# Turning the second heads of attention pairs right behind the first ones, in idle matmul banks of a one-core transformer kernel

## The chip, the cores and the metric

The kernel runs on 1 core of one Trainium2 chip. The metric is the device time of one execution in microseconds (us); that of a kernel is the median of several executions. TensorE, VectorE (DVE), ScalarE (ACT), GpSimd (POOL) and SyncE (SP) each take their own instructions strictly in order and meet at semaphores.

## The reference, cut to what matters

Three transformer layers at 256 tokens and width 2048, all in float32. The first block has a mixer (gated MLP, dilated attention, sparse attention), attention to a memory, and an MLP. The second block has two layers (l = 0, 1), and the change is in their mixers:

```python
proj = h @ w_in[l]                      # qa ka va qb kb vb qc kc vc, heads of 64
oa = window_attention(...)              # 8 heads, bias by distance, a sink
ob = neighborhood_attention(...)        # 8 heads, bias by position
oc = axial_global_attention(...)        # 16 heads, rotary, no bias
mix = concat(rmsnorm(oa), rmsnorm(ob), rmsnorm(oc))
x = x + mix @ w_o[l]
# then x = x + relu(rmsnorm(x) @ w_up)**2 @ w_down
```

Each attention is softmax(q k^T + bias) v. Heads are handled in pairs: 4 pairs of branch A, 4 of B and 8 of C in each layer.

## The kernel before, in words

A plan, `make_plan`, lists all steps in one order (`p.steps`), and every engine's program walks this list and issues its own part of each step. So the order of steps is the order of each engine's queue.

**Units.** The weights (600 MB) stream from HBM in halves of 128 x 1024 floats into five buffers `wt`. For exactness each half is split: ACT copies the high part to `wh` (L2173), VectorE forms the low part `wl` (L2435). TensorE multiplies: for each of 16 weight tiles one matmul with `wh` over 512 columns (high and low parts of the activations) and one with `wl` over 256. Sixteen such tiles are a unit, 32 matmuls. A unit adds up in one of three PSUM banks (0 to 2), taken in turn by `next_bank`; bank `banks["n"] % 3` is the next unit's. At the start of the next unit the sum is taken out: ACT copies one half of the bank to `tA`, VectorE adds the other into `tB`, GpSimd multiplies by the norm. Then the splits for the unit after follow. So the queues of ACT and VectorE hold, per unit: the sum of the last unit, two splits, and then the stage of attention.

**Order of units in a layer's mixer** (`ORDER2`): 4 value units `va`; tiles 26, 27 (keys of C); 18 to 25 (queries of C); 4 value units `vb`; tiles 4 (key of A), 0, 1, 2, 3 (queries of A), then 6, 10, 7, 11, 8, 12, 9, 13 (queries and keys of B in turn: tile 6+i is `qb` i, tile 10+i is `kb` i). A value unit holds two banks through all its four units. Then 8 units of two parts with the first half of `w_o`, and 8 with the second.

**Attention in the background.** Each pair is a generator, `two_heads`. `step_bg` runs at the eighth weight tile of a unit and lets each generator do one step, oldest pair first: load the biases (A and B alone, when two `sS` buffers are spare; there are six), two units of waiting, `score2`, then `prob`, then the turning, then `av`, in one unit each. At most one pair scores in a stage. In `score2` TensorE writes the scores of both heads, VectorE takes row maxima (L2579 for C, L2446 with the bias for A and B), ACT the exponentials (L2269, L2258). In `prob` VectorE takes a reciprocal and multiplies (L2595, L2439). Turning is four TensorE transposes of 128 x 128 for a head (L1827) and a copy of the bank to `sP`: on ACT for the first head (L2173), on VectorE for the second (L2749). `av` is the product with the values, eight matmuls of `sP`.

**Where the second head waits.** There is one bank for turning, `bP` (bank 5). So the first head is turned in the stage at tile 8, and the second is put into `late`, which runs at tile 13 of the same unit. Until the norm of C is formed, the second heads of A and B take `bM` (bank 7) instead.

```python
turn_head(hds[0], pts[0], 0)
late.append(lambda: turn_head(hds[1], pts[1], 1))
```

**B's masks.** A bias of B comes by eight small DMAs for a pair, issued by SP (L1810), and GpSimd adds a mask to it (L2794, `sS<-sS,c`), four instructions a pair, at the place of the bias step.

**The norm of C.** `across` forms it between two units: sums over the channels at tile 13 of one unit, then at tile 3 of the next one TensorE spreads the result over the bank `bM` and VectorE copies it to `rB`. Until then no sum of a unit is taken out (`held["evac"]`). The norm of the memory in the first block goes the same way.

Of the kernel before, what the change touches and what calls it, by code (L numbers as in the profile page):

```python
# [53 lines left out]
class Plan:  # L54
# [9 lines left out]
    def step(self, *what):  # L64
        self.steps.append(what)
# [76 lines left out]
def make_plan():  # L142

    p = Plan()
# [91 lines left out]
    held = {"evac": False, "s1": 0}  # L236

    late = []
# [40 lines left out]
    def run_at13():  # L279
        while at13:  # L280
            at13.pop(0)()
# [8 lines left out]
        else:  # L290
            step("mm", h, k, k + 1)

    banks = {"n": 0, "held": set()}

    def next_bank():

# [51 lines left out]

    def unit_end():
        run_at13()  # L350
        while after_unit:
            after_unit.pop(0)()

# [19 lines left out]
    def unit(parts, nk, src, thin=False, stages=(8,), ahead=2, early=False, tail=False):  # L373

        u = unit_begin(ahead)
        n = 0
        for j, (first, last, ev) in enumerate(parts):
            if first:
                next_bank()
            g = len(groups) - 1  # L380
            for k in range(nk):
                marks(n, None if len(parts) == 1 else max(1, 4 - n // 4) if thin else 0, stages, early)
                if (thin or tail) and n == 11:
                    run_pending()
                h = where[2 * u + n // 8][1]
                end = last and k == nk - 1
                if thin:
                    half = 2 * k // nk
                    tiles[h].append((g, src(j, k % (nk // 2)), k % (nk // 2) == 0, end, half, (k + 1) % (nk // 2) == 0))
                else:  # L390
                    tiles[h].append((g, src(j, k), first and k == 0, end, None, end))
                matmuls(h, n % 8)
                if n % 8 == 7:
                    done[g] = tick("t_used", h)
                    give(("wh", h % 4), done[g])
                elif end:
                    done[g] = tick("t_thin", g)
                n += 1
            if last:
                pending.append((ev, g))  # L400
                if j < len(parts) - 1:
                    kept = pending.pop()
                    run_pending()
                    pending.append(kept)
        unit_end()
        return done[g]

# [27 lines left out]
    def value_unit(name, ev, stages=(8,), ahead=2, early=False):  # L435

        v = VALUES[name]
        u = unit_begin(ahead)
        if name not in open_values:
            gs = next_bank(), next_bank()  # L440
            banks["held"] |= {p.bank[g] for g in gs}
            open_values[name] = [*gs, 0]
        g0, g1, k = open_values[name]
        n = 0
        for c in range(2):
            h = where[2 * u + c][1]
            for i in range(v.depth):
                for q in range(2):
                    for _ in range(4 // v.depth):
                        marks(n, None, stages, early)  # L450
                        n += 1
                    step("vmm", h, (g0, g1)[q], q, src_x(k), i, v.width, k == 0, k == KT - 1, (c, i, q) == (c, v.depth - 1, 1))
                k += 1
            done[g0] = done[g1] = tick("t_used", h)
            give(("wh", h % 4), done[g1])
        open_values[name][2] = k
        if k == KT:
            del open_values[name]
            banks["n"] = 3 - p.bank[g0] - p.bank[g1]
            pending.append((ev, (g0, g1)))  # L460
        unit_end()
        return done[g1]
# [106 lines left out]
    def across(begin, end):  # L569

        kept = {}

        def first():
            kept["b"] = begin()
            held["evac"] = True

        def second():
            end(kept["b"])
            held["evac"] = False
            run_pending()  # L580
        at13.append(first)
        after_unit.append(lambda: at3.append(second))

    def end_T(b, scale=None, keep=False):
        norm_end(b, "rT", scale, keep)
# [553 lines left out]

    sS_of, qden, branch_norms = {}, {}, set()  # L1140

    def turn_head(hd, pt, j):
        s = sS_of[hd]
        apart = j == 1 and hd[1] in "AB" and (hd[0], "C") not in branch_norms
        bank = "bM" if apart else "bP"
        step("turn", hd, s, pt, j, apart)
        take(bank, bank, *hd)
        take(("Pt", pt), "Pt", *hd)
        give(("S", s), tick("t_turn", *hd))
        sS.held.discard(s)  # L1150
        give(bank, tick("v_pcopy" if j else "a_pcopy", *hd))

    def av_heads(pr, parts):
        step("av", pr, tuple(parts))
# [37 lines left out]
    def two_heads(pr, qk, v, bias=False, sink=False):  # L1192

        hds = [(*pr, j) for j in range(2)]
        if bias:
            while sS.spare() < 2:
                yield
            for hd in hds:
                s = sS_of[hd] = sS.grab()
                step("bias", hd, s)  # L1200
                take(("S", s), "S", *hd)
                if hd[1] == "B":
                    tick("g_mask", *hd)
            yield
            yield
        else:
            while not has("g_rope", *qk[0], 1):
                yield
            yield
        while (held["s1"] >= 1 or dens.spare() < 4 or not (bias or sS.spare() >= 2)  # L1210
               or not all(has("g_proj", *x) or has("v_rdone", *x) or has("g_rope", *x, 1) and x[0] == "qc" for x in qk)):
            yield
        held["s1"] += 1
        ds = [dens.grab() for _ in hds]
        dq = None if bias else qden[qk[0][1]]
        if not bias:
            for hd in hds:
                s = sS_of[hd] = sS.grab()
                take(("S", s), "S", *hd)
        step("score2", pr, tuple(sS_of[hd] for hd in hds), tuple(ds), bias, sink, dq)  # L1220
        for j, (hd, d) in enumerate(zip(hds, ds)):
            take(("bS", j), "bS", *hd)
            take(("den", d), "den", *hd)
            tick("t_score", *hd)
            if bias:
                tick("v_max", *hd, 0)
                give(("bS", j), tick("v_max", *hd, 1))
                if sink:
                    tick("v_max", *hd, 2)
            else:  # L1230
                tick("v_max", *hd, 0)
                tick("v_max", *hd, 1)
            for n_ in range(3 if sink else 2):
                tick("a_exp", *hd, n_)
            if not bias:
                give(("bS", j), ("a_exp", at["a_exp", *hd, 1]))
        if dq is not None:
            give(("den", dq), ("a_exp", at["a_exp", *hds[1], 1]))
            dens.held.discard(dq)
        yield  # L1240
        for hd, d in zip(hds, ds):
            prob_ticks(hd, d, sink)
        yield
        while sP.spare() < 2:
            yield
        pts = [sP.grab() for _ in hds]
        turn_head(hds[0], pts[0], 0)
        late.append(lambda: turn_head(hds[1], pts[1], 1))
        yield
        while not has("a_v", *v):  # L1250
            yield
        av_heads(pr, [(hds[j], pts[j], j, v) for j in range(2)])
# [150 lines left out]
    for l in range(2):  # L1403
# [90 lines left out]
        for t in ORDER2:  # L1494
# [3 lines left out]
            if t >= 26:  # L1498
                ev = rope_tile("kc2", t - 26, G_QK2 + 2 + l, 64.0 ** -0.5)
            elif t >= 18:  # L1500
                ev = rope_tile("qc", t - 18, G_QK2 + l, None)
            elif t >= 10:
                ev = project("kb", (l, t - 10), free="o2")
            elif t >= 6:
                ev = project("qb", (l, t - 6), "Q", free="o2")
            elif t == 4:
                ev = project("ka", (l, 0), free="o2")
            else:
                ev = project("qa", (l, t), "Q", free="o2")
            last_in = unit([(True, True, ev)], KT, X2)  # L1510
            if 18 <= t < 26:
                pair("C", t - 18)
            elif t == 4:
                for br in "AB":
                    for i in range(4):
                        pair(br, i)
# [38 lines left out]
def program(nc, I, out):  # L1555
    p, feed, tiles, done = make_plan()
    at, free = p.at, p.free
    with ExitStack() as ctx:
# [261 lines left out]
        def _(eng):  # L1820
# [254 lines left out]
                    t = mm(bS[b][:, qt * T:(qt + 1) * T], q[b0:b0 + n, qt * P:(qt + 1) * P], k[b0:b0 + n, 0:T], True, True)  # L2075
                t.then_inc(S.t_score)

            def prob_turn(hd, s, pt, odd, apart):
                w.wait_ge(S.v_prob, at["v_prob", *hd])
                bank = bM if apart else bP  # L2080
                let_go(w, "bM" if apart else "bP", *hd)
                for kt in range(2):
                    for qt in range(2):
                        t = turn(bank[:, kt * T + qt * P:kt * T + (qt + 1) * P], sS[s][:, qt, kt * P:(kt + 1) * P])
# [346 lines left out]
        def _(eng):  # L2431
# [183 lines left out]
            for kind, *key in p.steps:  # L2615
# [126 lines left out]
                elif kind == "prob":  # L2742
                    prob(*key)
                elif kind == "turn" and key[3]:
                    hd, s, pt, _, apart = key
                    bank = bM if apart else bP
                    w.wait_ge(S.t_turn, at["t_turn", *hd])
                    let_go(w, "Pt", *hd)
                    eng.tensor_copy(sP[pt][:, :, :], bank[:, 0:512].rearrange("p (a b) -> p a b", a=2)).then_inc(S.v_pcopy)  # L2749
# [338 lines left out]
```

## Time and profile before

| | |
|---|---|
| median of 3 runs | 3294.0 us (3291.27 to 3294.38) |
| the profiled execution | 3291.06 us, span in the profile 3289.3 us |
| TensorE busy | 99% of the span, granted clock 0.999 |
| VectorE, ACT, GpSimd busy | 66%, 49%, 28% |
| DMA | 604.55 MB, mean 184 GB/s |
| C stretch, first layer | about 1257 to 1337 us |
| C stretch, second layer | about 2295 to 2373 us |
| the A and B tiles behind it | 1337 to 1429, 2373 to 2464 us |

All times in the rows are microseconds from the start of the span, unless marked ns. A busy TensorE isn't TensorE at its peak: matmuls overlap, and their ends are modelled, so the starts are the better measure. "[0.51 <-DVE sP L2749]" at a row's end says that the engine was idle for 0.51 us ahead of it and what ended that.

### The profile page before, as it was taken

The page shows a single profiled execution, that of the slowest core. Times are in us where ns is not written, and L with a number is a line of the kernel's source. Part 1 is how long each engine was busy: PE and PEld are TensorE (multiplying, and loading weights), DVE is VectorE, ACT ScalarE, POOL GpSimd, SP SyncE. Part 2 cuts the span into 40 slices and gives each one's busy share as a digit, 9 for nine tenths or more (in the row PEclk, how much of TensorE's full clock was granted, in tenths as well). Part 3 has the DMA queues.
Part 4 walks back from the last instruction along what each step waited for, and adds up shares of the span by engine and source line. Part 5 has one row for each costly group of instructions (what it writes and reads, how often), then busy time and mean ns, then how long its engine had stood idle before and what let it go on. Part 6 is the DMA issues. An engine that isn't in the chain of part 4 may idle for free.

```text
span 3289.3 us, 48362 instructions
## 1 busy us (share of the span) xinstructions
PE 3261.1 (99%) x19088; PEld 2854.0 (87%) x19088; DVE 2174.3 (66%) x3068; ACT 1621.1 (49%) x2692; POOL 915.6 (28%) x821
## 2 busy tenths in 40 slices
PE   8999999999999999999999999999999999999998
PEld 7989888888888897788888888889788888888887
DVE  6668687754676668778764477555778775457654
ACT  5457454443444545555443344444655544344443
POOL 2434133210232224255320033112336331013221
PEclk9999999999999999999999999999999999999999
DMA  7544546756655553555565566555355565555554
GB/s 259 189 165 149 176 157 216 230 191 191 191 189 193 185 188 132 161 168 184 192 192 193 186 188 190 194 190 178 125 176 170 187 190 195 190 186 190 189 193 145
DMA packets 188279, 604.55 MB, mean 184 GB/s; under 512 B 36597, under 2 KB 41573, under 8 KB 188054
## 3 DMA queue, kind: packets, MB, share of 16 engines
q1 hardware_dynamic: 188054, 601.47, 56.8%
q8 instruction: 151, 2.47, 0.3%
q14 instruction: 74, 0.61, 0.1%
HBM read 599.16 MB, written 8.00 MB: 185 GB/s over the span
## 4 chain that ended last, share of the span: by engine, by line
PE 91%; DVE 5%; ACT 2%; issue 1%; POOL 0%; DMA 0%; DVEq 0%; POOLq 0%; SPq 0%; ACTq 0%
PE ps L1824 90%; DVE wl L2435 3%; ACT sS L2269 1%; PE ps L1827 1%; DVE x L2443 1%; ACT wh L2173 1%; DVE xr L2435 1%; DVE sS L2439 1%; DVE den L2579 0%; ACT tA L2173 0%; DMA wt<-in_w_in 0%; POOL acc L2794 0%; DVE ua L2443 0%; POOL qc L2794 0%; ACT tG L2426 0%
## 5 line engine op out<-in xcount | busy, mean ns | idle before, releaser
L2435 DVE TENSOR_TENSOR wl<-wt,wh 128x1024 fp32r<-128x1024 f32 (+2 forms) x1104 | 1469.1, 1363 | 311.5 <-ACT wh L2173 295.5
L1824 PE MATMUL ps<-x,wh 128*128 128x512 f32 x4448 | 1561.8, 393 | 11.8 <-DVE x L2443 9.8
L1824 PE MATMUL ps<-x,wl 128*128 128x256 f32 x4448 | 1254.5, 282 | 0.0
L2173 ACT ACTIVATE wh<-wt 128x1024 fp32r<-128x1024 f32 (+2 forms) x1104 | 1117.8, 1051 | 275.0 <-PE ps L1824 235.8
L1824 PEld LDWEIGHTS ps<-x,wh 128*128 128x128 f32 x4448 | 836.1, 188 | 192.3 <-DVE wl L2435 12.8
L1824 PEld LDWEIGHTS ps<-x,wl 128*128 128x128 f32 x4448 | 841.8, 189 | 0.6
L1824 PE MATMUL ps<-ua,wh 128*128 128x512 f32 (+1 forms) x2432 | 832.0, 386 | 0.0
L1824 PE MATMUL ps<-ua,wl 128*128 128x256 f32 x2368 | 667.4, 282 | 0.0
L2435 DVE TENSOR_TENSOR tB<-ps,tA 128x256 f32<-128x256 f32 x422 | 177.1, 423 | 724.1 <-ACT tA L2173 723.9
L2173 ACT ACTIVATE tA<-ps 128x256 f32<-128x256 f32 x422 | 158.8, 380 | 943.0 <-PE ps L1824 942.8
L1824 PE MATMUL ps<-ub,wh 128*128 128x512 f32 x1536 | 536.6, 390 | 0.0
L1824 PEld LDWEIGHTS ps<-ua,wh 128*128 128x128 f32 x2432 | 452.2, 188 | 92.7 <-issue 1.4
L2794 POOL TENSOR_TENSOR tB<-tB 128x256 f32<-128x256 f32 x192 | 316.8, 1650 | 735.7 <-DVE tB L2443 735.7
L1824 PEld LDWEIGHTS ps<-ua,wl 128*128 128x128 f32 x2368 | 447.5, 189 | 0.2
L1824 PE MATMUL ps<-ub,wl 128*128 128x256 f32 x1536 | 433.1, 282 | 0.0
L2794 POOL TENSOR_TENSOR xr<-xr,tB 128x256 f32<-128x256 f32 x143 | 118.5, 831 | 858.2 <-DVE tB L2435 855.7
L1824 PEld LDWEIGHTS ps<-ub,wh 128*128 128x128 f32 x1536 | 288.3, 188 | 60.4
L1824 PEld LDWEIGHTS ps<-ub,wl 128*128 128x128 f32 x1536 | 290.3, 189 | 0.0
L2794 POOL TENSOR_TENSOR acc<-acc,tS 128x256 f32<-128x256 f32 x122 | 153.1, 1255 | 111.5 <-ACT tS L2178 102.5
L1824 PE MATMUL ps<-wh,x 128*128 128x512 f32 (+3 forms) x512 | 145.5, 358 | 0.5 <-DVE wl L2435 0.5
L1824 PEld LDWEIGHTS ps<-wh,x 128*128 128x128 f32 x512 | 91.8, 188 | 13.6 <-issue 2.1
L1824 PE MATMUL ps<-wl,x 128*128 128x512 f32 (+3 forms) x256 | 90.4, 353 | 0.0
(233 smaller groups left out, 1843.2 us busy)
## 6 DMA issues: line engine op xcount, KB each, us to landing
wt<-in_w_up SPq DMA_DIRECT2D x384, 512.0 KB, 4.4
wt<-in_w_down SPq DMA_DIRECT2D x384, 512.0 KB, 4.7
wt<-in_w_in SPq DMA_DIRECT2D x156, 512.0 KB, 4.6
wt<-in_w_o SPq DMA_DIRECT2D x64, 512.0 KB, 4.5
wt<-in_w_out SPq DMA_DIRECT2D x32, 512.0 KB, 4.5
wt<-in_w_vb SPq DMA_DIRECT2D x16, 512.0 KB, 4.0
wt<-in_w_va SPq DMA_DIRECT2D x16, 384.0 KB, 3.7
wt<-in_w_vsl SPq DMA_DIRECT2D x8, 512.0 KB, 6.2
```

The lines of the kernel that those rows point to most:

```text
L1824: return eng.matmul(o, l, r, start=start, stop=stop, skip_group_check=True)
L1827: return eng.transpose(o, i, idt[0:n, 0:n])
L2173: return eng.activation(o, i, ACT.Copy, **kw)
L2269: eng.activation(sS[s][:, qt, :], bS[b][:, qt * T:(qt + 1) * T], ACT.Exp, bias=nm[:, qt:qt + 1], scale=scale, accum_out=dn[:, qt:qt + 1]). ...
L2435: return eng.tensor_tensor(o, a, b, op)
L2439: return eng.tensor_scalar(o, a, s1, None, op0)
L2443: return eng.scalar_tensor_tensor(out=o, in0=a, scalar=s, in1=b, op0=op0, op1=op1, **kw)
L2794: return eng.tensor_tensor(o, a, b, op)
```

## The change

Four things. The second head is turned in the same stage, directly behind the first, if `idle_bank` finds one of the three matmul banks that neither the open unit nor a sum not yet taken out occupies. It finds none while sums are held back (`evac`), in units of two parts, and in unit 25, which stands ahead of value units (`fresh`); then the second head goes into `late` as before. For A and B it looks first at the next unit's bank, for C first at the one after that, which is the last unit's. The copy by VectorE then reads that bank, and the bank's next user waits for this copy. Last, the second half of `across` runs at tile 5 instead of tile 3.

```diff
+    def idle_bank(older):
+
+        if held["evac"] or banks["open"] is None or banks["fresh"]:
+            return None
+        busy = set(banks["open"])
+        for _, g in pending:
+            busy |= {p.bank[i] for i in (g if isinstance(g, tuple) else (g,))}
+        left = [(banks["n"] + j) % 3 for j in ((1, 0, 2) if older else (0, 1, 2)) if (banks["n"] + j) % 3 not in busy]
+        return left[0] if left else None
...
     def unit_end():
         run_at13()
+        banks["open"] = None
...
+            banks["open"] = (p.bank[g],) if len(parts) == 1 else None
...
+        banks["open"] = (p.bank[g0], p.bank[g1])
...
         at13.append(first)
-        after_unit.append(lambda: at3.append(second))
+        after_unit.append(lambda: at5.append(second))
...
-    def turn_head(hd, pt, j):
+    def turn_head(hd, pt, j, b=5):
         s = sS_of[hd]
-        apart = j == 1 and hd[1] in "AB" and (hd[0], "C") not in branch_norms
-        bank = "bM" if apart else "bP"
-        step("turn", hd, s, pt, j, apart)
-        take(bank, bank, *hd)
+        bank = {5: "bP", 7: "bM"}.get(b, ("main", b))
+        step("turn", hd, s, pt, j, b)
+        take(bank, "turn", *hd)
         take(("Pt", pt), "Pt", *hd)
         give(("S", s), tick("t_turn", *hd))
         sS.held.discard(s)
         give(bank, tick("v_pcopy" if j else "a_pcopy", *hd))
+
+    def second_turn(hd, pt):
+        b = idle_bank(hd[1] == "C")
+        if b is not None:
+            turn_head(hd, pt, 1, b)
+        else:
+            late.append(lambda: turn_head(hd, pt, 1, 7 if hd[1] in "AB" and (hd[0], "C") not in branch_norms else 5))
...
         turn_head(hds[0], pts[0], 0)
-        late.append(lambda: turn_head(hds[1], pts[1], 1))
+        second_turn(hds[1], pts[1])
...
+            banks["fresh"] = t == 25
             last_in = unit([(True, True, ev)], KT, X2)
+            banks["fresh"] = False
```

## Rows read from the trace of the kernel before

**Rows 1.** The page: the span, and TensorE's busy time, share and instructions.
```profile
span 3289.3 us, 48362 instructions
...
PE 3261.1 (99%) x19088; PEld 2854.0 (87%) x19088; DVE 2174.3 (66%) x3068; ACT 1621.1 (49%) x2692; POOL 915.6 (28%) x821
```

**Rows 2.** TensorE's waits over the whole span: us in total, times, longest.
```profile
PE ps L1824 <- DVE sP L2749: 0.9, 2, 0.5
PE ps L1827 <- ACT sP L2173: 0.7, 2, 0.4
```

**Rows 3.** Timeline of TensorE, C stretch: start, us, operation [idle before <-releaser].
```profile
1284.56 1.08 PE L1824 MATMUL ps<-sP,vc 128*64 128x256 f32 x4
1286.15 1.08 PE L1824 MATMUL ps<-sP,vc 128*64 128x256 f32 x4 [0.51 <-DVE sP L2749]
...
1295.47 1.81 PE L1824 MATMUL ps<-sP,vc 128*64 128x256 f32 x8
...
1325.04 1.09 PE L1824 MATMUL ps<-sP,vc 128*64 128x256 f32 x8
...
1337.71 0.63 PE L1827 MATMUL ps<-idt,sS 128*128 128x128 f32 x4 [0.36 <-ACT sP L2173]
```

**Rows 4.** The chain of waits in order of time: start, us, what.
```profile
1287.15 0.96 ACT wh L2173
1288.13 2.98 DVE wl L2435 x2
...
1297.27 0.96 ACT wh L2173
...
1333.39 1.16 ACT vb L2173 x2
...
1343.77 1.75 PE ps L1824 x10
1345.52 0.44 PE ps L1827 x4
```

**Rows 5.** Timeline of VectorE, end of the C stretch.
```profile
1339.64 0.68 DVE L2749 COPY sP<-ps 128x512 f32<-128x512 f32 x1
1340.24 0.41 DVE L2435 TENSOR_TENSOR tB<-ps,tA 128x256 f32<-128x256 f32 x1
```

**Rows 6.** Timeline of TensorE, value products of A0 and A3.
```profile
1377.83 1.59 PE L1824 MATMUL ps<-sP,va 128*64 128x256 f32 x8
...
1416.01 1.88 PE L1824 MATMUL ps<-sP,va 128*64 128x256 f32 x8
```

**Rows 7.** Timeline of VectorE, units 6 and 10.
```profile
1377.60 0.69 DVE L2749 COPY sP<-ps 128x512 f32<-128x512 f32 x1
...
1380.49 2.51 DVE L2435 TENSOR_TENSOR wl<-wt,wh 128x1024 fp32r<-128x1024 f32 x2 [0.53 <-ACT wh L2173]
```

**Rows 8.** Timeline of SP's DMA issues, biases of B0 and B2.
```profile
1387.86 6.33 SPq L1810 DMA_DIRECT2D sS<-rpm  x8
...
1420.26 5.20 SPq L1810 DMA_DIRECT2D sS<-rpm  x8
```

**Rows 9.** Timeline of GpSimd, masks of the same pairs (B0: second head).
```profile
1396.43 1.23 POOL L2794 TENSOR_TENSOR sS<-sS,c 128x256 f32<-128x256 f32 x2 [0.64 <-DMA sS<-rpm]
...
1425.06 3.52 POOL L2794 TENSOR_TENSOR sS<-sS,c 128x256 f32<-128x256 f32 x4 [4.57 <-DMA sS<-rpm]
```

**Rows 10.** Timeline of TensorE, the spread of C's norm.
```profile
1438.50 0.63 PE L1824 MATMUL ps<-idt,den 128*128 128x128 f32 x4
```

**Rows 11.** Timeline of VectorE, the read of C's norm.
```profile
1440.02 0.42 DVE L2483 COPY rB<-ps 128x256 f32<-128x256 f32 x1
```

**Rows 12.** Timeline of VectorE, prob products with GpSimd idle and while it masks.
```profile
1365.24 0.62 DVE L2439 TENSOR_SCALAR sS<-sS,den 128x256 f32<-128x256 f32 x2
...
1404.51 1.14 DVE L2439 TENSOR_SCALAR sS<-sS,den 128x256 f32<-128x256 f32 x2
```

**Rows 13.** Busy time, C stretch: length, each engine, clock, DMA share, GB/s.
```profile
1257.90:1337.70 79.80, 78.66 (x437) 59.67 (x437) 62.11 (x137) 49.38 (x119) 30.15 (x32) 1.00 0.34 113
```

More of the change, by code:

```diff
@@ L291, in matmuls @@
             step("mm", h, k, k + 1)
-    banks = {"n": 0, "held": set()}
+    banks = {"n": 0, "held": set(), "open": None, "fresh": False}
+    def idle_bank(older):
[6 more added lines that the diff above has]
+        return left[0] if left else None
     def next_bank():
@@ L2076, in score, with prob_turn @@
                 t.then_inc(S.t_score)
-            def prob_turn(hd, s, pt, odd, apart):
+            def prob_turn(hd, s, pt, odd, b):
                 w.wait_ge(S.v_prob, at["v_prob", *hd])
-                bank = bM if apart else bP
-                let_go(w, "bM" if apart else "bP", *hd)
+                bank = ps[:, b, :]
+                let_go(w, "turn", *hd)
                 for kt in range(2):
@@ L2744, in _ @@
                 elif kind == "turn" and key[3]:
-                    hd, s, pt, _, apart = key
-                    bank = bM if apart else bP
+                    hd, s, pt, _, b = key
+                    bank = ps[:, b, :]
                     w.wait_ge(S.t_turn, at["t_turn", *hd])
```

## The prediction

> **What bounds the kernel now.** I read the page first: TensorE is busy for 99% of the span [rows 1], so time comes or goes only where TensorE waits or is given other work. The matmul work is the same after the change, so I looked for waits. The view of TensorE's waits gives the copies of turned heads (`sP`) 1.6 us in two rows, over both layers [rows 2]. That understates them, because matmul ends are modelled. The timeline shows more: the eight matmuls of a value product take 1.09 us where all is ready (1325.04), but four of them took 1.59 us (1284.56 to 1286.15), against half of that, and eight took 1.81 us at 1295.47 [rows 3]. So some 1.1 and 0.7 us were lost waiting for the second head's copy on VectorE, which stands at the end of VectorE's stage. These are the waits that the change goes at.
>
> The second thing to see is the chain of waits through the C stretch, about 1257 to 1337 us. It doesn't run through TensorE. It goes round ACT and DVE: first half of `wh` at 1287.15, both `wl` at 1288.13, then the prob products, the row maxima, the exponentials, and the next `wh` at 1297.27 [rows 4]. One round is 10.1 us and nothing in it waits for TensorE; both engines take their instructions in order. It ends in the copies of `vb` (1333.39 to 1334.55) and, after `wh`, the copy of a turned head, for which TensorE's turning at 1337.71 waits [rows 3]. TensorE has nearly as much work per round as the loop is long, so it is 99% busy and still follows the loop.
>
> **The change, part by part.** I call a unit by its tile number. Pair Ci scores in unit 22+i for i up to 3, then in the four `vb` units; it is turned two units later and multiplied with its values three units later.
>
> 1. *Turning itself.* No instruction is added. Four turns between weight matmuls take 0.44 us in the chain [rows 4], and eight in a row should take twice that; I count 0.
>
> 2. *The second head's copy on VectorE, C pairs.* Before, it came after the row maxima, while ACT did exponentials: outside the loop. Now its step stands before the prob products and maxima of younger pairs, so it is inside. Two instructions after each other show its price: 1339.64 to 1340.24, 0.60 us [rows 5]. An idle bank is found for pairs 0, 2, 3, 4, 5 before the last exponentials of the stretch (pair 1 is held back in unit 25): 5 x 0.60 = 3.0 us on the loop. TensorE gains the lost waits of value products but runs into the loop again: turning pair 6 in unit 4 takes a bank that has just held `vb`, and must wait for the copies of `vb`. These now end at 1334.55 + 3.0 = 1337.55. Then four turns 0.44 and ten matmuls 1.75 with 0.09 for the switch [rows 4] bring TensorE to 1339.8, where it was at 1338.1 (1337.71 and 0.4 for the turns). That is +1.7 us a layer. Bounds: -0.4 (only the wait of 0.36 goes [rows 3]) and +2.1 (five copies at their whole 0.68 [rows 5]).
>
> 3. *Waits of value products, A and B pairs.* The product of A0 takes 1.59 us (1377.83), that of A3 1.88 (1416.01) [rows 6]; 1.09 would do, and the next group starts 0.07 before its end. Both wait for a copy that VectorE reaches late (1377.60 [rows 7]). With the copy ahead of the prob products both go: -0.5 - 0.8 = -1.3 us. Bounds: 0 and -1.3.
>
> 4. *The bank taken.* For A and B the idle bank is the next unit's, so the next unit's first matmul waits for the copy. Behind A1 (unit 10) that bites. TensorE: turning at 1377.83 + 1.02 = 1378.85, two heads 0.88, 16 matmuls 2.8 with 0.1 [rows 4], so unit 7 could start at 1382.6. VectorE: `wl` at 1380.49, pushed by A0's copy to 1381.1, ends 1383.6 [rows 7], and the copy behind it at 1384.2. Wait: +1.6 us. For the other pairs the copy is in time by the same count, by only 0.4 us for A0. Bounds: 0.6 (no push, and VectorE's `wl` at its shortest) and 2.5.
>
> 5. *What else the turn gives back.* An `sS` buffer is free in the plan once its head is turned. Now both of a pair's are free in the same stage, before younger pairs are asked, so from A3 on each bias load, score, prob and turn comes one unit earlier. B3's bias is loaded in unit 12 instead of 13, and its masks on GpSimd stand ahead of the product of key tile `kb` 2, for which B2's score in unit 9 waits. SP may issue these loads when B0 is turned in unit 12. From SP's first issue to the last mask's end it took 8.3 us once (1420.26 to 1428.58) and 9.8 once (1387.86 to 1397.66) [rows 8, 9]; the key's product adds 0.74. TensorE needs 2.8 + 2.8 + 1.0 + 0.9 = 7.5 us from that turn to B2's score. So it waits 8.3 + 0.74 - 7.5 = 1.5 to 3.0 us. I take 1.6, near the short end, since the shorter row is from the units nearest to it. Bounds: 0, if the key is formed in time, and 3.0. Below the masks nothing is saved, since the scores are only moved.
>
> 6. *The norm's spread at 5 instead of 3.* In the C norm it was on TensorE at 1438.50, and VectorE read it at 1440.02, behind `wl` [rows 10, 11]. Two tiles (0.7 us) later it ends at about 1439.6, still ahead of the read. Cost 0; if that cover were gone, 0.7 us of evacuation, still ahead of the bank's next use. The norm of the memory lies the same way.
>
> Per layer: +1.7 - 1.3 + 1.6 + 1.6 = +3.6; two layers +7.2 us. The profiled execution took 3291.1 us (span 3289.3 and 1.8 around it), so +7.2 makes 3298.3. It lies 2.9 below the median of the runs, 3294.0; on that the forecast is 3301.
>
> One rule bears on item 5. Two prob products of one head take 0.62 us at 1365.24 and 1.14 us at 1404.51, where GpSimd was masking [rows 12]. The Trainium skill, page SBUF — State Buffer, section "SBUF: two separate sides", says that VectorE and GpSimd share a port pair, which is held for a whole instruction while the other is fully blocked; this trace agrees in direction. By it the masks, coming one unit earlier, would slow other VectorE work instead. The number of masks stays, and I add nothing.
>
> **The rivals.**
> *A: the loop is not lengthened.* VectorE has idle time in each round, and if the copy fills it, waits vanish and nothing comes for them. For it: DVE is busy for only 62 of 80 us in the stretch [rows 13]. Against it: the chain has no gap in which it could hide. It gives -1.1 - 0.7 - 0.4 in the C stretch and -1.3 after it, -3.5 a layer, 3287. It decides for faster from the point where items 4 and 5 together cost under 1.8 us a layer.
> *B: TensorE's new waits are hidden.* The loop is longer, but the key comes in time and the bank is free nearly in time (0.6): 1.7 - 1.3 + 0.6 = +1.0 a layer, 3296.
> *C: all terms at their upper ends.* 2.1 - 1.3 + 2.5 + 3.0 = +6.3 a layer, 3307.
> *D: the change does nothing.* No idle bank is found or the plan is the old one. The code excludes it for single-tile units.
>
> **How the numbers follow.** What a measurement here can tell from no change is 0.2%, 6.6 us. The forecast (+3 to +11 us) has 0.48, A (3283 to 3291) 0.17, B (3291 to 3297) 0.27, C 0.08. The range reaches from half of A to C: 3288 to 3307; the likeliest case alone has 3297 to 3305. A is faster in most of its span, with a little for what I have not seen: 0.17. Slower by over 0.2% is C and two thirds of the forecast's case: 0.41. The rest, 0.42, is within.
>
> **What would show it.** Loop: rounds in the C stretch of 10.7 instead of 10.1 us, `vb` copies 3 us later against the stretch's start. Item 2: value products of 1.02 us, and turning of pair 6 behind the copies of `vb`. Item 4: a gap ahead of unit 7's first matmul, released by the copy. Item 5: A3's score one unit earlier and a gap ahead of B2's score, released by GpSimd. The prediction is wrong if VectorE's order lets the copy slip beside the exponentials, if `wl` gets shorter because fewer of them meet GpSimd, or if the bias loads land faster with a less crowded queue.

## The result and the profile after

The changed kernel takes 3306.08 us (median of 5 runs, 3304.92 to 3309.68), the kernel before 3294.0 (5 runs beside it, 3291.27 to 3294.52). The ratio is 1.004, interval 1.0029 to 1.0051: slower. The forecast was 3301. 3306 lies in the range of 3288 to 3307, but near its upper end, and beyond 3297 to 3305, the range of the likeliest case. "Within 0.2%" had been given 0.42 and "slower" 0.41, so, by the forecast's own threshold of 0.2%, the likelier of these two did not happen.

The profiled execution took 3306.08 us, 15.0 more than the profiled one of before. The page of the changed kernel, for [rows 1]:

```profile
span 3304.3 us, 48374 instructions
...
PE 3260.5 (99%) x19088; PEld 2855.8 (86%) x19088; DVE 2171.9 (66%) x3068; ACT 1620.4 (49%) x2692; POOL 910.4 (28%) x821
```

The matmuls are the same in number, and summed over the kernel their busy time is too, so all 15 us show as gaps. Not all of it was caused by waits: the groups of value products are 8.2 us shorter in all (44.1 before, 35.9 after), and other groups are longer by about as much, in part where the granted clock was low. The view of TensorE's waits, for [rows 2] (us in total, times, longest):

```profile
PE ps L1845 <- DVE x L2464: 9.9, 2, 9.0
PE ps L1845 <- POOL kb L2815: 8.0, 4, 3.4
PE ps L1845 <- DVE sP L2770: 4.1, 5, 1.7
PE ps L1848 <- DVE tB L2456: 3.8, 2, 2.9
PE ps L1845 <- DVE wl L2456: 2.4, 4, 0.8
PE ps L1848 <- ACT vb L2194: 2.4, 2, 1.2
```

Of these the first and the fifth were there before as well. New are the waits for keys that GpSimd forms (`kb`, 8.0), more waits for the VectorE copy (`sP`, 4.1), one in each layer for the last unit's sum (`tB`, 3.8), and pair 6's for `vb` (2.4). In place of [rows 3] and [rows 6], the timeline of TensorE:

```profile
1276.68 0.60 PE L1848 MATMUL ps<-idt,sS 128*128 128x128 f32 x4
1280.14 1.09 PE L1848 MATMUL ps<-idt,sS 128*128 128x128 f32 x4 [2.86 <-DVE tB L2456]
1281.16 2.09 PE L1845 MATMUL ps<-kc,qc 64*128 64x256 f32 x8
...
1289.55 1.09 PE L1845 MATMUL ps<-sP,vc 128*64 128x256 f32 x8
...
1337.45 0.66 PE L1848 MATMUL ps<-idt,sS 128*128 128x128 f32 x4
1339.29 0.63 PE L1848 MATMUL ps<-idt,sS 128*128 128x128 f32 x4 [1.18 <-ACT vb L2194]
...
1381.09 1.09 PE L1845 MATMUL ps<-sP,va 128*64 128x256 f32 x8
...
1387.65 0.47 PE L1845 MATMUL ps<-x,wh 128*128 128x512 f32 x1 [1.67 <-DVE sP L2770]
...
1409.39 1.14 PE L1845 MATMUL ps<-kb,qb 64*128 64x256 f32 x8 [1.14 <-POOL kb L2815]
...
1416.21 1.09 PE L1845 MATMUL ps<-sP,va 128*64 128x256 f32 x8
...
1428.30 1.14 PE L1845 MATMUL ps<-kb,qb 64*128 64x256 f32 x8 [2.39 <-POOL kb L2815]
...
2464.62 1.09 PE L1848 MATMUL ps<-idt,sS 128*128 128x128 f32 x8
2469.09 2.09 PE L1845 MATMUL ps<-kb,qb 64*128 64x256 f32 x8 [3.37 <-POOL kb L2815]
```

The value products are at 1.09 where they took 1.6 to 1.9 before: what the change goes at, it gets. In return each of the new waits stands where a step of the prediction had put one, and two stand where none had: the second turn of pair 0 at 1280.14, and the score at 1409.39 (key tile 1). Two of the scores also take 2.09 instead of 1.14 us. There the granted clock was at the lower of its two levels, 1.2 instead of 2.4 GHz. The view of the windows (length, busy us of PE, PEld, DVE, ACT, POOL, then the granted clock, DMA share, GB/s):

```profile
496.00:500.00 4.00, 3.35 (x11) 2.99 (x12) 3.61 (x6) 1.19 (x2) 0.90 (x2) 0.50 0.46 157
...
1280.00:1284.00 4.00, 3.86 (x17) 2.75 (x18) 3.45 (x5) 1.92 (x3) 1.05 (x2) 0.57 0.20 27
...
2464.00:2468.00 4.00, 1.72 (x16) 1.03 (x12) 1.97 (x3) 1.15 (x3) 2.12 (x4) 1.00 0.71 134
2468.00:2472.00 4.00, 2.91 (x11) 2.10 (x12) 0.84 (x5) 0.37 (x1) 1.67 (x3) 0.50 0.74 304
2472.00:2476.00 4.00, 4.00 (x17) 3.43 (x17) 0.63 (x4) 1.83 (x9) 0.00 (x0) 0.65 0.01 2
```

A stretch at clock c loses its length times (1 - c), if TensorE sets the pace there: the last two rows 4 x 0.50 + 4 x 0.35 = 3.4 us.

To place the rest I took the same instruction in both traces and subtracted the times. This is the lag behind the kernel before, in us, for all kernels of this study, under the names that they have in the experiments below; the column heads are the second C score of the layer's mixer (start of C in layer 0), the last C value product, the first C score of layer 1, its last C value product, the last matmul that reads `wh`, and the end of the span. All 14 come from one profiled execution each.

```
              C0 start  C0 end  C1 start  C1 end  last wh   end
before (at)    1267.6   1349.7   2297.5   2385.4   3275.4  3289.3
after             1.9      3.3      6.5      7.4     14.5    15.0
norm3             2.6      3.2      8.1      8.9     14.0    14.6
hold_s            1.2      2.6      5.1      5.9      8.1     9.1
hold_bank         0.8      2.2      3.7      4.5      6.4     7.2
best3             0.8      1.5      3.3      3.5      5.4     5.9
ab_only           0.0      0.0      3.3      3.3      8.9     9.3
a_only            1.7      1.7      2.6      2.6      3.5     3.5
b_only            0.2      0.3      1.3      1.3      2.3     3.3
c_only            0.3      1.7      1.7      2.5      2.7     3.1
c_not24           1.4      2.1      2.1      2.3      2.5     2.5
c_late            1.2      3.5      4.3      5.3      5.4     5.4
c_1to4            1.6      3.1      3.5      4.4      4.6     5.0
c_1to5            1.0      3.1      3.0      4.5      4.6     4.5
```

So of the changed kernel's 15.0 us, C took 1.4 and 0.8 in the two layers, A and B 3.3 and 7.1. The end of the kernel, behind the last weights, took 0.5; it varies from 0 to 1.0 among these executions and is no part of A and B. The 1.9 ahead of the mixer of layer 0 is no part of the change's cost: there the clock fell at 492 to 504 us, which it did in 7 of the 14 profiled executions (after, norm3, hold_s, a_only, c_not24, c_late, c_1to4), and these came 1.2 to 2.6 late, the others 0 to 1.0. The five runs of the kernel before also fall into two groups, 3291.3 to 3291.7 and 3294.0 to 3294.5.

### The profile page after: what moved, and what is told of

Read it like the earlier page. It is cut to its first block, busy times and chain, and to the rows that moved or that the text cites. A ratio compares the mean times of both kernels' runs of the same rounds, so it can differ in the third digit from the quotient of the medians.

```text
span 3304.3 us, 48374 instructions
## 1 busy us (share of the span) xinstructions
PE 3260.5 (99%) x19088; PEld 2855.8 (86%) x19088; DVE 2171.9 (66%) x3068; ACT 1620.4 (49%) x2692; POOL 910.4 (28%) x821
## 4 chain that ended last, share of the span: by engine, by line
PE 87%; DVE 6%; ACT 4%; issue 2%; POOL 1%; DMA 0%; SPq 0%; DVEq 0%; POOLq 0%; ACTq 0%
PE ps L1845 86%; DVE wl L2456 3%; ACT wh L2194 1%; ACT sS L2290 1%; DVE sS L2460 1%; ACT sS L2279 1%; PE ps L1848 1%; POOL acc L2815 0%; DVE x L2464 0%; DVE xr L2456 0%; DVE den L2600 0%; DVE sP L2770 0%; ACT tA L2194 0%; DMA sS<-rpm 0%; DVE sS L2467 0%
```

## The experiments

The kernel before, run again beside the experiments, had medians of 3292.1 to 3292.7 (15 to 33 runs each). All are the changed kernel with the edit shown.

### One part undone: held buffers, and the norm

```diff
     def second_turn(hd, pt):                        # hold_s
...
             turn_head(hd, pt, 1, b)
+            s = sS_of[hd]
+            sS.held.add(s)
+            late.append(lambda: sS.held.discard(s))
```

> The changed kernel, but a second head's buffer `sS` counts as free in the plan only at tile 13, as in the kernel before; the turn itself stays early. Theory (step 5 of the prediction, mis-sized): the waits for key tiles 1 and 2 behind GpSimd's masks (1.1 and 2.4 us in layer 0, 1.2 and 3.4 in layer 1) go, and with them the half-clock stretch behind the last one; 3306 - 8 - 2 = about 3296. Rival (steps 2 and 4, the VectorE copy on the loop and the bank waits are the cost, step 5 costs nothing): 3303 or more.

Measured: 3298.78 us, ratio 1.002 (1.0011 to 1.0029). 7.3 us of the 13.6 are gone (the changed kernel's 3306.1 less 3292.5, the kernel before in its largest set, 33 runs), and the four waits for `kb` with them. The theory's sum said 10. What it missed is in the waits of hold_s. The first matmul of the unit behind A1 still waits for the copy, as in the changed kernel. With the scores back at their old places, the units behind A3 and B0 wait for it too (the second and third row), which the key waits had hidden.

```profile
1386.92 0.47 PE L1848 MATMUL ps<-x,wh 128*128 128x512 f32 x1 [1.65 <-DVE sP L2773]
...
1417.74 0.47 PE L1848 MATMUL ps<-x,wh 128*128 128x512 f32 x1 [0.63 <-DVE sP L2773]
...
1426.59 0.47 PE L1848 MATMUL ps<-x,wh 128*128 128x512 f32 x1 [1.02 <-DVE sP L2773]
```

By the table A and B now take 2.5 and 2.2 us, instead of 3.3 and 7.1: in layer 0 the key waits of 3.5 us cost 0.8 net, in layer 1 those of 4.5 us cost 4.9, of which 3.4 was the clock.

```diff
-        after_unit.append(lambda: at5.append(second))
+        after_unit.append(lambda: at3.append(second))      # norm3
```

> The changed kernel with the third branch's norm spread back at tile 3. Theory (step 6: free): 3306 within 2. Rival (the later spread costs the 1.9 us by which the changed kernel is later before layer 0's mixer, or frees or delays something at the branch end): 3303 or less.

Measured: 3305.68 us, ratio 1.004 (1.0028 to 1.0053), 0.4 under the changed kernel. The later spread is free, as said. Its trace serves for the clock. Here it fell in layer 0 behind a wait of 2.36 us, where the changed kernel's wait of 2.39 at the same instruction left it up. From norm3, TensorE's timeline and the windows:

```profile
1428.28 1.56 PE L1845 MATMUL ps<-kb,qb 64*128 64x256 f32 x8 [2.36 <-POOL kb L2815]
```

```profile
1424.00:1428.00 4.00, 1.92 (x16) 1.16 (x13) 1.91 (x3) 1.15 (x3) 3.21 (x5) 1.00 0.81 215
1428.00:1432.00 4.00, 3.72 (x15) 2.81 (x16) 1.47 (x8) 1.75 (x7) 0.86 (x2) 0.61 0.54 217
1432.00:1436.00 4.00, 4.00 (x24) 3.51 (x23) 1.06 (x2) 2.34 (x5) 0.74 (x1) 0.96 0.00 0
```

That is 4 x 0.39 + 4 x 0.04 = 1.7 us, and A and B take 8.1 - 3.2 = 4.9 there, 1.6 more than in the changed kernel.

### One part alone: C, A, B

```diff
-        b = idle_bank(hd[1] == "C")
+        b = idle_bank(True) if hd[1] == "C" else None          # c_only
+        b = None if hd[1] == "C" else idle_bank(False)         # ab_only
+        b = idle_bank(False) if hd[1] == "A" else None         # a_only
+        b = idle_bank(False) if hd[1] == "B" else None         # b_only
```

> Early second turns for the third branch (C) alone; A's and B's are turned at tile 13 as before. Theory: C's own cost is the wait in unit 24 with its half-clock stretch and pair 6's wait for copies, less the value product waits: +1.4 in layer 0 and +0.9 in layer 1, so 3294 + 2.3 = about 3296 (3294 to 3299). Rival (the loop of ACT and VectorE lengthened by the copies is the main cost): 3300 or more.

> Early second turns for branches A and B alone; C's at tile 13 as before. Theory: A and B carry the main cost, +3.9 in layer 0 and +7.9 in layer 1: 3294 + 9 to 12 = 3303 to 3306. Rival (C's turns are the main cost): 3298 or less.

Measured: c_only 3294.63 us, ratio 1.0007 (0.9999 to 1.0016), 2.5 above the kernel before. ab_only 3301.67, ratio 1.0029 (1.0018 to 1.004), 9.6 above it. These fit the expected 2.3 and 9 to 12 above the kernel before. Together they are 12.1 of the 13.6, so the two nearly add up, and about three quarters belong to A and B.

> Early second turns for branch A alone. Theory of step 5 (A's freed buffers bring A3's score and B1's forward, and their keys are late behind the masks on GpSimd): A's early turns carry the key waits, 1.1 and 2.4 us or more in layer 0, and the copy wait of 1.7 a layer; 3299 to 3302, most of the 9.6 of A and B together. Rival (B's turns free the buffers that matter): 3294 to 3296, no key wait above 0.5.

> Early second turns for branch B alone. A's alone cost 2.0 us (3294.7), A's and B's together 9.6 (3301.7). Theory (the wait for key tile 2 needs both: A's early turns bring the scores forward and B's bring B3's buffers, biases and masks in front of that key on GpSimd): B alone costs little, 0 to 3 us, 3292.5 to 3295.5, and no score waits over 1 us for a key. Rival (B's early turns put the masks in front of the key by themselves): 3297 to 3300, with the wait of 2 to 3 us in both layers.

Measured: a_only 3294.70 us, ratio 1.0006 (0.9997 to 1.0015), 2.0 above. b_only 3294.50, ratio 1.0005 (0.9996 to 1.0014), 1.9 above. Neither interval is clear of 1, but both are far below the 9.6 of A and B together. So my theory for a_only fell: A's early turns bring the wait for key tile 1 (1.22 in layer 0, 0.94 in layer 1) and the copy wait of 1.66, but most of the 9.6 us isn't theirs. The rival there was wrong about the key wait, right about the time. The theory for b_only held: it has no wait for a key, and the wait for key tile 2 needs both. The wait for key tile 1 has another cause than the theories gave. In the changed kernel GpSimd had finished its masks and stood idle until VectorE's sum of that unit came; the score had moved up to where its key was only being formed:

```profile
1408.56 0.73 POOL L2815 TENSOR_TENSOR kb<-tB,rT 128x256 f32<-128x256 f32 x1 [3.41 <-DVE tB L2456]
```

For key tile 2 GpSimd's timeline shows the masks. In a_only the key (1421.97) comes before the masks of B3 (1428.41 and 1430.53):

```profile
1421.97 1.65 POOL L2815 TENSOR_TENSOR kb<-tB,rT 128x256 f32<-128x256 f32 x1 [1.42 <-DVE tB L2456]
...
1428.41 1.23 POOL L2815 TENSOR_TENSOR sS<-sS,c 128x256 f32<-128x256 f32 x2 [3.13 <-DMA sS<-rpm]
```

In the changed kernel all four masks of B3 stand in front of it (for [rows 9]), and the load that they wait for is issued one unit earlier than before, right behind B0's turn. GpSimd's timeline, and SP's of both layers (for [rows 8]):

```profile
1424.79 2.73 POOL L2815 TENSOR_TENSOR sS<-sS,c 128x256 f32<-128x256 f32 x4 [2.57 <-DMA sS<-rpm]
1427.48 0.72 POOL L2815 TENSOR_TENSOR kb<-tB,rT 128x256 f32<-128x256 f32 x1
```

```profile
1418.89 5.20 SPq L1831 DMA_DIRECT2D sS<-rpm  x8
...
2458.68 5.20 SPq L1831 DMA_DIRECT2D sS<-rpm  x8
```

### The bank, and unit 24

```diff
-        b = idle_bank(hd[1] == "C")
+        b = idle_bank(True)                        # hold_bank: hold_s and this
...
-            banks["fresh"] = t == 25
+            banks["fresh"] = t in (24, 25)         # c_not24: c_only and this; best3: all three
```

> The kernel with the held buffers (3298.8), and A's and B's second turns go to the bank that the unit after the next takes, as C's do, so that the next unit's first matmul doesn't wait for the copy. Theory (step 4): of the waits for that copy, 5.9 us in all over the kernel before, four of 1.0 to 1.7 and one of 0.6 go; 3298.8 less 5 to 6 = 3293 to 3294. Rival (the waits come back at another place, the other bank being still read by the last unit's sum): 3297 or more.

Measured: 3298.74 us, ratio 1.0017 (1.0008 to 1.0026), the same as hold_s. The rival held. The waits for the copy fall from 6.8 to 1.1 us in all, but the other bank has not been read yet when the turn wants it, and the turns now wait for the last unit's sum, 8.9 us in all instead of 3.9. TensorE in hold_bank:

```profile
1373.24 0.63 PE L1851 MATMUL ps<-idt,sS 128*128 128x128 f32 x4 [0.46 <-DVE tB L2459]
...
1382.87 0.63 PE L1851 MATMUL ps<-idt,sS 128*128 128x128 f32 x4 [0.56 <-DVE tB L2459]
...
1413.22 0.63 PE L1851 MATMUL ps<-idt,sS 128*128 128x128 f32 x4 [1.47 <-DVE tB L2459]
```

Its profiled execution has shorter A and B stretches (1.5 and 1.9 us, against 2.5 and 2.2) and no clock fall before the last units, but its median is not below that of hold_s.

> Early second turns for the third branch alone, but not in unit 24 either, where pair 0 is turned while the last unit's sum is still due. Theory (the wait of 2.9 us for that sum with the half-clock stretch behind it, and 1.0 in layer 1, is C's cost; elsewhere C gains the value product waits less pair 6's): 3294.6 of the third-branch kernel less 4 to 5 = 3290 to 3291, 1 to 2 under the kernel before. Rival (C's cost is the copies on the loop of ACT and VectorE, step 2): no gain over 3294.6.

Measured: 3293.92 us, ratio 1.0002 (0.9993 to 1.0011), 0.7 under c_only, which is not clear of noise, where 4 to 5 were expected. The theory fell. By the table C takes 1.4 and 0.8 us with the early turn in unit 24 and 0.8 and 0.2 without, and that difference of 0.6 is the copy on the loop, not the wait: the round of ACT at this place takes 10.09 us in c_only and 9.50 in c_not24, as in the kernel before. ACT in c_only and in c_not24:

```profile
1277.83 2.00 ACT L2194 ACTIVATE wh<-wt 128x1024 fp32r<-128x1024 f32 x2
1287.92 1.99 ACT L2194 ACTIVATE wh<-wt 128x1024 fp32r<-128x1024 f32 x2
```

```profile
1278.91 2.00 ACT L2194 ACTIVATE wh<-wt 128x1024 fp32r<-128x1024 f32 x2
1288.41 1.99 ACT L2194 ACTIVATE wh<-wt 128x1024 fp32r<-128x1024 f32 x2
```

TensorE's wait of 2.9 us itself is made good within the next units, where the value products no longer wait: in c_only the lag behind the kernel before is 3.9 us right behind it and 0.8 by 1300 us. A clock fall of 1.7 us there is absorbed as well. c_only had one behind this wait and hold_bank had none; yet both are 1.4 us later at the end of C than at its start. In a_only it fell at 1280 us with no early turn near, and the lag was 1.7 before and after. norm3 lost 3.4 us there, and C took 0.6. TensorE is not what sets the pace in this stretch.

> All three edits: held buffers, the other bank for A and B, no early turn in unit 24. If the three costs add up: 3293.5 less 4 to 5 = 3289, which is 3 under the kernel before (the value product waits of A0, A3 and C go and nothing comes in their place but pair 6's 1.2 us). If they hide one another: 3292 or more.

Measured: 3296.85 us, ratio 1.0012 (1.0003 to 1.0021). The waits hide one another: with all three edits the early turns are still 4.3 us worse than none, as the second of the two expectations (3292 or more) had it.

### C: the copies on the loop

```diff
         give(("S", s), tick("t_turn", *hd))
...
-        give(bank, tick("v_pcopy" if j else "a_pcopy", *hd))
+        def copied():                              # c_late: c_only and this
+            if j:
+                step("copy2", hd, pt, b)           # VectorE's part alone
+            give(bank, tick("v_pcopy" if j else "a_pcopy", *hd))
+        if b in (5, 7):
+            copied()
+        else:
+            late.append(copied)
```

> Early second turns for the third branch alone, in the same units, but only TensorE's part is early: VectorE's copy of the second head stays at tile 13. Theory of step 2 (the early copies lengthen the loop of ACT and VectorE and make pair 6's turn wait for copies of vb, 1.2 us a layer): pair 6's wait falls to 0.4 or less, about 1.7 us a layer less, 3291 to 3293; the value products wait again as in the kernel before if the late copy is what held them, which would take some 1.3 to 3 back. Rival (the loop isn't lengthened by the copies): pair 6 still waits 1.2 and the time stays at 3294.6 or goes above it.

Measured: 3294.99 us, ratio 1.0005 (0.9996 to 1.0014), not below c_only. Neither the theory nor the rival has both right: the mechanism is there, the time is not. ACT's timeline shows the loop. The changed kernel, for [rows 4]:

```profile
1299.67 2.00 ACT L2194 ACTIVATE wh<-wt 128x1024 fp32r<-128x1024 f32 x2
1310.41 2.00 ACT L2194 ACTIVATE wh<-wt 128x1024 fp32r<-128x1024 f32 x2
...
1337.87 1.27 ACT L2194 ACTIVATE vb<-ps,den 128x512 f32<-128x512 f32 x2
```

and c_late:

```profile
1299.93 2.00 ACT L2201 ACTIVATE wh<-wt 128x1024 fp32r<-128x1024 f32 x2
1309.54 2.00 ACT L2201 ACTIVATE wh<-wt 128x1024 fp32r<-128x1024 f32 x2
...
1335.74 1.27 ACT L2201 ACTIVATE vb<-ps,den 128x512 f32<-128x512 f32 x2
```

From the `wh` of this round to the copies of `vb` it is 38.2 us with the copies early and 35.8 with them late; before it was 1333.4 - 1297.3 = 36.1 [rows 4]. So four early copies (of pairs 2 to 5) put 2.1 us on the loop. In four rounds they added 0.6, 0.6, 0.3 and 0.6, by ACT's timelines of both kernels. Pair 6's wait for `vb` is gone from c_late's waits. What probably eats the gain: this execution had the longest clock fall of all at 1276 to 1292 us (0.88, 0.50, 0.50 and 0.84 in four windows of 4 us, 5.1 us lost), so its layer 0 can't be compared with the others as a whole; and in layer 1 the bank is wanted before the late copy has read it:

```profile
2372.53 0.47 PE L1852 MATMUL ps<-x,wh 128*128 128x512 f32 x1 [1.38 <-DVE sP L2777]
```

Last, I tried to keep the part of C in which the lag had shrunk (from 1.3 to 0.3 us over pairs 0 to 4 in c_not24, before it grew to 2.1):

```diff
+        b = idle_bank(True) if hd[1] == "C" and 1 <= hd[2] <= 4 else None      # c_1to4; c_1to5: <= 5
```

> Early second turns for pairs 1 to 4 of the third branch alone. In the kernel with all but pair 0 early (3293.9) the lag behind the kernel before fell by 1.0 us from pair 1 to pair 4 in layer 0 and by 1.5 in layer 1, and grew by 1.8 in each from pair 5 on, where the second turn waits for copies of vb. Theory: the growth goes, the gain stays, 2.5 us under the kernel before: 3289 to 3291 against 3292.5. Rival (the 1.8 is only work moved back to its place, owed anyway once the early turns stop): 3292 to 3294.

> The same with pair 5 early too, whose copy the next unit's first matmul waits 0.3 us for. Theory (pair 5 costs 0.3 to 0.9 a layer by its copy on the loop and that wait, pair 6 the rest): 0.6 to 1.8 above the run of pairs 1 to 4. Rival (only pair 6 costs): no more than 0.3 above it.

Measured: c_1to4 3295.36 us, ratio 1.001 (1.0001 to 1.0019); c_1to5 3298.08, ratio 1.0015 (1.0007 to 1.0024). My theory fell: stopping early doesn't keep the gain. With pair 5 the median is 2.7 above that of pairs 1 to 4, more than the 0.6 to 1.8 expected; the two profiled executions don't show this difference, since that of c_1to5 was its fastest run (3295.6). TensorE is ahead only for a few units, and meets the longer loop at the next place where it needs a copy. In c_1to4 that is the late turn of pair 6, which waits for ACT's copy; in c_1to5 it is the same one with a longer wait:

```profile
1340.81 0.63 PE L1848 MATMUL ps<-idt,sS 128*128 128x128 f32 x4 [1.37 <-ACT sP L2194]
```

```profile
1340.82 0.63 PE L1848 MATMUL ps<-idt,sS 128*128 128x128 f32 x4 [2.46 <-ACT sP L2194]
```

No version here beats the kernel before.

## Why the prediction was off

The sum was +7.2 us, measured +12 beside it and +13.6 against the later runs of before. The costs that the forecast named are all in the trace. The step that failed is the size of item 5, the waits for keys: 3.5 and 4.5 us were measured where 1.6 a layer was put in. The lowered clock behind the longest of these waits, 3.4 us, was not in the sum at all.

- *Item 1, turning itself: right.* Eight turns take 1.02 to the next group.
- *Item 2, copies on the loop, +1.7 a layer: right in mechanism, in size for layer 0 alone.* C took 1.4 and 0.8 us (also in c_only). A round with an early copy takes 10.74 us (1299.67 to 1310.41), where the same round took 10.14 before, as forecast (10.7). Counted from the start of C, the `vb` copies come 2.7 us later (3.0 forecast), and pair 6's turn waits 1.18 for them. c_late confirms it from the other side. In layer 1 the `vb` copies come 8.7 us later than before (2377.65 against 2368.97) where C began 6.5 later, 2.1 of its own. Rival A, that the copies fill idle time, is thereby excluded in both layers. I did not see that pair 0's turn, in unit 24, would wait 2.86 us for a sum; it made no difference to the time, and the 0.6 a layer that c_not24 saves is pair 0's copy on the loop.
- *Item 3, the value products of A0 and A3, -1.3 a layer: right,* at 1381.09 and 1416.21, where both end after 1.02 us.
- *Item 4, the bank, +1.6: right, in part by luck.* The wait ahead of unit 7 is 1.67 and 1.64 us. But "for the other pairs the copy is in time" held only because the key waits came first: in hold_s, without them, the waits for the copy are 3.3 and 2.7 us.
- *Item 5, +1.6 a layer, upper bound 3.0: too small.* First, a wait was missed: A3's early turn brings B1's score forward too, and key tile 1, held up by VectorE's sum and not by masks, is late for it by 1.14 and 1.15 us. Second, the wait for key tile 2 is 2.39 and 3.37 us. From the end of B0's turn (1418.25) to the score (1428.30) it took 10.05 us: 0.64 until SP issued, 8.63 from there to the last mask's end, 0.78 for the key. I had 8.3 and 0.74, from the shorter of two rows, and nothing between turn and issue. In layer 1 the same path took 11.04 (0.63, 9.6 and 0.8); the longer row, 9.8, was the one to take there. TensorE's 7.5 us between them was right (7.67). So item 5 was 3.5 and 4.5 us instead of 1.6. With items 3 and 4 that makes 3.8 and 4.8 a layer; measured without the clock, 3.3 and 3.7.
- *Not in the sum: the clock.* Behind the 3.37 us wait in layer 1 the granted clock fell and took 3.4 us. With it A and B make 7.1 us of that layer in the table. In ab_only it was 1.7 us at the same place, and 5.6 less 1.7 is 3.9, much the same.
- *Item 6, the norm, 0: right* (norm3).

By layer the forecast had 3.6 and 3.6, of which A and B 1.9 each; the trace has 4.7 and 7.9, A and B 3.3 and 7.1. Rival C had the time (3307) but not the cause: its bank and loop terms were not at their upper ends. That slower and within were given equal chances follows from the same step: with 3.5 and 4.5 for item 5 the sum is +12, the forecast 3306, and most of its case slower by over 0.2%. The count for "faster" was loose as well: 0.2% under 3294 is 3287.4, so only half of A's 3283 to 3291 lies below it, and by A's own -3.5 a layer "faster" would have needed items 4 and 5 to cost under 0.2 us a layer, not 1.8.

Open: whether hold_bank gains anything over hold_s. Its profiled execution is 1.9 us shorter, but that of hold_s lies 1.5 above hold_s's own median. Open too is how the longer loop of c_not24 (its `vb` copies come 2.1 and 1.5 us later, counted from the start of C) leaves only 0.8 and 0.2 us at the end of C; the executions differ by as much in where the clock falls.

## What to carry to other kernels

When a step is moved forward, price each resource that it frees as well: here the turns were cheap, and the buffers they gave back pulled loads, masks and scores ahead of the keys they needed, which made up 7 of the 14 us lost, the lowered clock behind them included. A load that starts at a release is costed from that release to the last consumer's end, queue and issue included, and with the longer of the rows seen, not the shorter. Waits that look additive hide one another: undoing 10 us of them returned 7, moving 6 us of copy waits to another bank returned nothing, and a gain of 1 us ahead of a loop that sets the pace was handed back at its next copy.

## What the runs showed of the hardware

The granted clock fell from 2.4 to 1.2 GHz behind stops of TensorE of 2.4 to 3.4 us, in the middle of a kernel that is 99% busy, and it did so in some executions and not in others at the same instruction: behind 2.36 us in norm3 but not behind 2.39 in the changed kernel; behind 2.86 there, but not behind 2.87 in hold_bank. In a_only it fell at 1280 us (0.57 in the window of 4 us) with no stop longer than 0.21 us shown just ahead. The length of the stop alone doesn't decide it, and what does is not shown by these traces. A fall took 1.7 to 5.1 us of TensorE's time. Where TensorE set the pace (the A and B units) it was paid in full (in layer 0 norm3 took 1.6 us more there than the changed kernel, for a fall of 1.7), and where ACT and VectorE did (C in layer 0) none of a fall of 1.7 us was left at the end of the stretch. So in layer 1 a wait of 3.4 us was followed by as much again.
